# One stream of expert rows through all steps, and three latent input blocks moved ahead of the context's attention in layer 1

## The chip, the cores and the metric

One core of a Trainium2 chip runs the whole kernel in one launch. The metric is device time in microseconds (us), lower is better. Engines are named as in the profile: PE (TensorE, its weight loads apart as PEld), DVE (VectorE), ACT (ScalarE), POOL (GpSimd), SP (SyncE, which here only issues transfers).

## The reference, cut to what matters

Two layers over five blocks of 128 tokens (block 0 is the context, 1 to 4 are latent tokens), all in float32. In each layer every block goes through an input projection, four groups of attention or mixing heads, an output projection, a normalisation, and then PEER, the part this case is about: each token is routed to 16 of 16384 experts in each of 8 heads, and two gathered vectors of 1024 numbers, u and v, are used per expert.

```
h = x * (1 + scale1) + shift1 ; z = h @ w_in ; mix in four head groups
x = LayerNorm(alpha * x + gate1 * (GroupRMSNorm(concat) @ w_out))
h = x * (1 + scale2) + shift2
  s   = (h @ peer_w_q) . sub_keys ; top 16 of 128 twice, top 16 of 256 sums -> eid, gate
  act = gelu(peer_u[eid] . h)                          # per token, head, expert
  y   = sum over heads and experts of gate * act * peer_v[eid]
x = LayerNorm(alpha * x + gate2 * y)
```

Context tokens see only context keys, latent tokens see the latent blocks and a cached context.

## The kernel before, in words

**Steps.** The program is a chain of steps, each a block of five engine programs that ends in a barrier of all engines which also clears the semaphores (`end_step`, L379). mod(L) computes the modulation of layer L, in(L,b) the input projection of block b, att(L,b) the attention, output projection and routing of block b. The order is written out by hand at the end of `build`: mod(0), in(0,0), att(0,0), then per layer in(L,1) to in(L,4), att(L,1) to att(L,4), and between the layers mod(1), in(1,0), att(1,0). After the last att stands a step of experts alone, then the last sum.

**Expert rows.** Work on the experts of block b of layer L (a job) is 256 rows: 8 heads with 16 u rows and 16 v rows. A row is one gather of 128 x 1024 numbers (512 KB), issued by POOL (L502), which lands in a slot. A u row is reduced against the block's x2 by DVE (L603); 16 of them make a head's dots, ACT takes the gelu (L538) and DVE the weights (`wsel`, L596). Of the v rows DVE adds the odd ones into `acc` (L613), and PE the even ones into two PSUM banks (L571) with a diagonal matrix that ACT writes (L545). So of 256 rows DVE handles 192 and PE 64.

**How rows are mixed into a step.** Each step is handed some rows of a job (class `Experts`), and each engine's program calls `rows(share)` at fixed places between its own instructions; there it handles rows up to that share of the step's rows, in 256ths. POOL calls it too, and issues gathers as many rows ahead as there are slots: 8 in mod and in (`RING`), 16 in att (`DEEP`, where 8 more lie in W). A gather waits until the row that held its slot has been used, by DVE or by PE. Engines run their programs in order, so a place in the program is also a place in a queue.

**Which rows in which step, before.** in(L,1) to in(L,4) take one head of job 0 each (32 rows), att(L,1) the other four heads (128 rows), att(L,2) to att(L,4) the whole of jobs 1 to 3 (256 rows each). Job 4 of layer 0 is spread over mod(1) (64), in(1,0) (32) and att(1,0) (160); that of layer 1 fills the step of experts alone (256). In steps with fewer than 8 heads the rows come in blocks (16 u, then 16 u and 16 v by turns); with 8 heads u and v rows alternate after the first 16 u rows, and the last 16 are all v. Every step starts with no row gathered and ends with all of its rows used. A job's last sum (`last_sum`, L434: ten DVE instructions) is run at the start of the next step that begins a job, at head 1 in att (`experts_vector_ended`).

Of the kernel before, what the change touches and what calls it, by code (L numbers as in the profile page):

```python
# [12 lines left out]
ds = bass.ds  # L13
# [48 lines left out]
DIAGS = 4  # L62

# [10 lines left out]
def row_order(heads, turn):  # L74


    u = [("u", h, k) for h in range(heads) for k in range(TOPK)]
    v = [("v", h, k) for h in range(heads) for k in range(TOPK)]
    order, u = u[:TOPK], u[TOPK:]
    while v:  # L80
        order += u[:turn] + v[:turn]
        u, v = u[turn:], v[turn:]
    return order


# [4 lines left out]
class Experts:  # L90

    def __init__(self, layer, block, first, heads, begin=False, end=False, ended=None, slots=RING, landings=None):
        self.layer, self.block, self.first, self.heads = layer, block, first, heads
        self.begin, self.end, self.ended = begin, end, ended  # L100
        self.order = row_order(heads, 1 if heads == PH else TOPK)

        self.by_dve, self.by_pe = [], []
        d = p = 0
        for kind, _, k in self.order:
# [7 lines left out]
        self.slots = slots  # L113
        self.count = []
        for r in range(len(self.order)):
            landings[r % slots] += 16
            self.count.append(landings[r % slots])

    def target(self, share):

        return min(len(self.order), len(self.order) * share // 256)

    def landed(self, n):

        return self.count[n]


def build(nc, a):
    es = ExitStack()
    with es:  # L130
# [55 lines left out]
        gates_e = sb("gates_e", [P, NSEL])  # L186
        eid_e = sb("eid_e", [P, NSEL], U32)
        eid_s = sb("eid_s", [P, 4, TOPK], U32)
# [158 lines left out]
        ids_in = sem("ids_in")  # L347
        e_in = sem("e_in")
        x2_copied = sem("x2_copied")
        ids_staged = sem("ids_staged")  # L350
        acc_zero = sem("acc_zero")
        used_dve = sem("used_dve")
        used_pe = sem("used_pe")
        gelu_sel = sem("gelu_sel")
        w_ready = sem("w_ready")
        diag_done = sem("diag_done")
# [9 lines left out]
        bias_stored = es.enter_context(nc.semaphore("bias_stored"))  # L366
        gath = [es.enter_context(nc.semaphore(f"gathered{i}")) for i in range(DEEP)]
        landings = [0] * DEEP

        def slot(E, r):  # L370

            i = r % E.slots
            return ring[:, i, :] if i < RING else W[:, KD * D + (i - RING) * D:KD * D + (i - RING + 1) * D]
# [44 lines left out]
        def experts_sync(sp, E):  # L418
            if E is not None and E.begin:
                sp.dma_start(eid_e[:, :], of_block(eid_dram, E.block)).then_inc(ids_in, 16)  # L420
                if E.ended is not None:
                    last_sum_in(sp, E.layer, E.ended, ended_tiles)
                sp.dma_start(x2e[:, :], of_block(x2_dram, E.block)).then_inc(e_in, 16)
                sp.dma_start(gates_e[:, :], of_block(gate_dram, E.block)).then_inc(e_in, 16)

        def last_sum_in(sp, layer, block, tiles):

            s = 0 if isinstance(block, int) and block == 0 else 1
# [5 lines left out]
        def last_sum(dve, tiles):  # L434

            link = chain(dve, end_chain)
            link(dve.tensor_tensor(acc[:, :], acc[:, :], acc_ps, ALU.add))
            dve.wait_ge(end_in, 64)
            link(dve.tensor_tensor(acc[:, :], acc[:, :], tiles[1], ALU.mult))
            link(dve.scalar_tensor_tensor(acc[:, :], tiles[0], ALPHA, acc[:, :], ALU.mult, ALU.add))  # L440
            layer_norm(link, dve, acc[:, :], tiles[2], tiles[3], tiles[0], st12e, mve, vee[:, :], rstde[:, :],
                       end_var, end_rstd, 1).then_inc(end_done, 1)
# [5 lines left out]
        def experts_sync_ended(sp, E):  # L448

            if E is not None and E.ended is not None:  # L450
                sp.wait_ge(end_done, 1)
                sp.dma_start(of_block(x_dram, E.ended), ended_tiles[0]).then_inc(end_stored, 16)

        def experts_gpsimd_ended(pool, E):
            if E is not None and E.ended is not None:
                last_sum_rstd(pool)

        def experts_vector_ended(dve, E):
            if E is not None and E.begin:
                if E.ended is not None:  # L460
                    last_sum(dve, ended_tiles)

                    dve.wait_ge(end_done, 1)

                dve.memset(acc[:, :], 0.0).then_inc(acc_zero, 1)

        def experts_sync_end(sp, E):
            if E is None:
                return
            if E.end:  # L470

                sp.wait_ge(used_dve, E.by_dve[-1])
                sp.wait_ge(used_pe, E.by_pe[-1])
                tiles = [ring[:, i, :] for i in range(4)]
                last_sum_in(sp, E.layer, E.block, tiles)
# [1151 lines left out]
```

## Time and profile before

| what | value |
|---|---|
| device time, median of 3 runs | 5282.86 us (5281.63 to 5284.09) |
| time of the profiled execution | 5288.4 us |
| its span, first to last instruction | 5286.6 us |
| busy share of the span | DVE 65%, PE 57%, POOL 53%, ACT 12% |
| gathers | 2560, 512 KB each |

No engine is busy all of the time: the steps are chains in which engines wait for one another. The table of steps among the rows below is the place to start. Its stretches are the steps, cut at the barrier between the last instruction of one step and the first of the next.

### The profile page before, as it was taken

The page shows a single profiled execution, that of the slowest core. Times are in us where ns is not written, and L with a number is a line of the kernel's source. Part 1 is how long each engine was busy: PE and PEld are TensorE (multiplying, and loading weights), DVE is VectorE, ACT ScalarE, POOL GpSimd, SP SyncE. Part 2 cuts the span into 40 slices and gives each one's busy share as a digit, 9 for nine tenths or more (in the row PEclk, how much of TensorE's full clock was granted, in tenths as well). Part 3 has the DMA queues.
Part 4 walks back from the last instruction along what each step waited for, and adds up shares of the span by engine and source line. Part 5 has one row for each costly group of instructions (what it writes and reads, how often), then busy time and mean ns, then how long its engine had stood idle before and what let it go on. Part 6 is the DMA issues. An engine that isn't in the chain of part 4 may idle for free. (4 is left out here: it accounts for less than half of the span.)

```text
span 5286.6 us, 34528 instructions
## 1 busy us (share of the span) xinstructions
PE 3032.0 (57%) x9560; PEld 1575.4 (30%) x9560; DVE 3434.8 (65%) x6877; ACT 633.4 (12%) x1577; POOL 2815.9 (53%) x2837
## 2 busy tenths in 40 slices
PE   7638766366356546547554676645554663565354
PEld 1423344134133223311232333423332331332111
DVE  1255467677776866773568555667686677769775
ACT  0101121120121111000110001111111201211000
POOL 1116645366466646644654564445664664665675
PEclk8768868678678767778777786777776886787676
DMA  8447778789899988989896878769898998998998
GB/s 337 159 184 247 250 281 339 292 334 390 309 346 356 352 328 329 393 313 368 325 361 259 307 242 305 286 259 348 343 377 316 337 391 305 339 358 345 355 404 322
DMA packets 439839, 1690.09 MB, mean 320 GB/s; under 512 B 53120, under 2 KB 66496, under 8 KB 427568
## 3 DMA queue, kind: packets, MB, share of 16 engines
q0 software_dynamic: 370528, 1353.39, 67.7%
q1 hardware_dynamic: 69120, 334.49, 16.4%
q8 instruction: 79, 1.29, 0.1%
q14 instruction: 112, 0.92, 0.1%
HBM read 1660.02 MB, written 33.95 MB: 320 GB/s over the span
## 5 line engine op out<-in xcount | busy, mean ns | idle before, releaser
L571 PE MATMUL ps<-ring,diag 128*128 128x512 f32 x1456 | 875.8, 747 | 844.8 <-ACT diag L545 748.7
L502 POOL DMA_INDIRECT ring<-in_peer_u,eid_s x728 | 785.8, 1079 | 596.0 <-DVE dots L603 360.0
L502 POOL DMA_INDIRECT ring<-in_peer_v,eid_s x728 | 737.8, 1013 | 487.1 <-PE ps L571 217.7
L502 POOL DMA_INDIRECT W<-in_peer_v,eid_s x552 | 570.4, 1033 | 349.7 <-issue 125.9
L571 PE MATMUL ps<-W,diag 128*128 128x512 f32 x1104 | 618.8, 698 | 234.2 <-DMA W<-in_peer_v,eid_s 164.6
L603 DVE CUSTOM_DVE_ANT_0 ring<-ring,ps 128x1024 f32<-128x1024 f32 x552 | 658.4, 1217 | 142.4 <-DMA ring<-in_peer_u,eid_s 139.5
L603 DVE CUSTOM_DVE_ANT_0 W<-W,ps 128x1024 f32<-128x1024 f32 x552 | 655.6, 1217 | 102.0 <-DMA W<-in_peer_u,eid_s 100.7
L571 PEld LDWEIGHTS ps<-ring,diag 128*128 128x128 f32 x1456 | 320.7, 235 | 1296.8 <-issue 1126.0
L502 POOL DMA_INDIRECT W<-in_peer_u,eid_s x552 | 540.5, 979 | 292.6 <-DVE dots L603 130.1
L613 DVE SCALAR_TENSOR_TENSOR acc<-ring,wsel,acc 128x1024 f32<-128x1024 f32 x364 | 474.2, 1303 | 99.1 <-DMA ring<-in_peer_v,eid_s 69.5
L613 DVE SCALAR_TENSOR_TENSOR acc<-W,wsel,acc 128x1024 f32<-128x1024 f32 x276 | 354.8, 1286 | 50.0 <-DMA W<-in_peer_v,eid_s 24.7
L571 PEld LDWEIGHTS ps<-W,diag 128*128 128x128 f32 x1104 | 224.3, 218 | 544.2 <-issue 295.8
L869 PE MATMUL ps<-W,hT 128*128 128x512 f32 (+1 forms) x800 | 324.2, 567 | 31.4 <-DVE hT L999 22.1
L1210 PEld LDWEIGHTS ps<-hT,W 128*128 128x128 f32 x2560 | 298.1, 193 | 49.6 <-issue 34.0
L1210 PE MATMUL ps<-hT,W 128*128 128x128 f32 x2560 | 300.6, 277 | 19.4 <-ACT hT L1267 10.4
L545 ACT ACTIVATE diag<-ident,wsel 128x128 f32<-128x128 f32 x640 | 229.0, 398 | 684.6 <-PE ps L571 427.9
L603 DVE CUSTOM_DVE_ANT_0 ring<-ring,x2e 128x1024 f32<-128x1024 f32 x176 | 219.1, 1283 | 87.7 <-DMA ring<-in_peer_u,eid_s 86.7
L493 POOL COPY eid_s<-eid_e 128x16 uint32<-128x16 uint32 x80 | 23.7, 296 | 414.2 <-DMA eid_e<-expert_ids 332.7
L1158 PE MATMUL ps<-ktB,xs 64*128 64x512 f32 x64 | 49.3, 1130 | 331.2 <-DMA xs<-spill_state 202.3
L869 PEld LDWEIGHTS ps<-W,hT 128*128 128x128 f32 x800 | 151.5, 203 | 193.3 <-issue 168.0
L750 PE MATMUL ps<-W,condS 128*2 128x512 f32 x384 | 173.2, 612 | 48.6 <-DMA toep<-in_b_ada 48.6
L1324 DVE SCALAR_TENSOR_TENSOR big<-ps,toep 128x512 f32<-128x512 f32 x32 | 22.1, 689 | 249.9 <-DMA band<-in_c_band 207.4
(212 smaller groups left out, 3311.5 us busy)
## 6 DMA issues: line engine op xcount, KB each, us to landing
W<-in_w_q SPq DMA_DIRECT2D x40, 2048.0 KB
W<-in_w_ada SPq DMA_DIRECT2D x24, 2048.0 KB
W<-in_w_out SPq DMA_DIRECT2D x10, 4096.0 KB, 30.5
W<-in_w_in SPq DMA_DIRECT2D x16, 2048.0 KB, 10.1
ring<-in_peer_u,eid_s POOLq DMA_INDIRECT x728, 6.7
ring<-in_peer_v,eid_s POOLq DMA_INDIRECT x728, 6.3
toep<-mod_rows SPq DMA_DIRECT2D x20, 512.0 KB, 8.7
aux<-mod_rows SPq DMA_DIRECT2D x19, 512.0 KB, 5.7
```

What stands on the lines that cost most here:

```text
L493: pool.tensor_copy(eid_s[:, h % 4, :], eid_e[:, ds((E.first + h) * TOPK, TOPK)]).then_inc(ids_staged, 1)
L502: pool.indirect_dma_start(slot(E, r), None, a["peer_u"] if kind == "u" else a["peer_v"], bass.IndirectOffsetOnAxis(ap=eid_s[:, h % 4, k:k ...
L545: act.activation(diag[:, n % DIAGS, :], ident[:, :], ACT.Copy, scale=wsel[:, h % 2, k:k + 1]).then_inc(diag_done, 1)
L571: last = pe.matmul(acc_ps[:, c * 512:(c + 1) * 512], diag[:, (E.by_pe[r] - 1) % DIAGS, :], slot(E, r)[:, c * 512:(c + 1) * 512], start=Fal ...
L603: dve.tensor_tensor_reduce(out=slot(E, r), in0=slot(E, r), in1=x2, scale=1.0, scalar=0.0, op0=ALU.mult, op1=ALU.add, accum_out=dots[:, h % ...
L613: dve.scalar_tensor_tensor(acc[:, :], slot(E, r), wsel[:, h % 2, k:k + 1], acc[:, :], ALU.mult, ALU.add).then_inc(used_dve, 1)
L750: last = pe.matmul(bank(c % NB, parts=2), condS[:, k, :], ada[:, c % NB, k, :], start=(k == 0), stop=(k == KD - 1))
L869: last = pe.matmul(bank(c, n), hT[:, k, :], w_in[c][:, k, :], start=(k == 0), stop=(k == KD - 1))
L1158: pe.matmul(near(i, lat), q, k[:, k0 * P:k0 * P + lat], start=True, stop=True)
L1210: last = pe.matmul(bank(2 + i % 2)[:, g * P:(g + 1) * P], w_q[c][:, k, g * P:(g + 1) * P], hT[:, k, :], start=(k == 0), stop=(k == KD - 1))
L1324: dve.scalar_tensor_tensor(sS[:, i % 2, 0:lat], near(i, lat), sc, bias, ALU.mult, ALU.add)
```

## The change

One stream holds the rows of all ten jobs, in one order for all: per job 16 u rows, then u and v by turns, then the last 16 v rows. A step takes a slice of the stream, and a slice may hold the end of one job and the start of the next. At a step's end POOL goes on and issues the gathers of the next 8 rows (16 from one att to the next, and into the step of experts alone), as far as their block is routed; these gathers are under way across the barrier, and their semaphores and counts are no longer cleared by it. The slots are handed out beforehand, to the row whose turn comes, least recently used first.

| step | rows before | rows now |
|---|---|---|
| in(0,1) to in(0,4) | 32 each | 40 each |
| att(0,1) | 128 | 80 |
| att(L,2) to att(L,4) | 256 each | 256 each, 16 rows behind the job |
| mod(1) | 64 | 72 |
| in(1,0) | 32 | 40 |
| in(1,1), in(1,2), in(1,3) | 32 each, of job (1,0) | 40 each, of job (0,4), between in(1,0) and att(1,0) |
| att(1,0) | 160 | 40 |
| in(1,4) | 32 | 40 |
| att(1,1) | 128 | 200 |
| experts alone | 256 | 272 |

The last sum is cut into pieces that stand between the rows behind the job's end. The zeroing of `acc` (a memset, four matmuls) goes: the first v rows of a job overwrite. POOL no longer copies a head's expert numbers to `eid_s`. In(1,1) to in(1,3) use the input weights that lie in W from in(1,0); in(1,4) now loads them, which in(1,1) did.

```diff
+class Stream:
+    JOB = PH * HEAD_ROWS
+    def __init__(self, jobs):
+        one = [("u", h, k) for h in range(PH) for k in range(TOPK)]
+        two = [("v", h, k) for h in range(PH) for k in range(TOPK)]
+        order = one[:LEAD]
+        for i in range(len(two)):
+            order += one[LEAD + i:LEAD + i + 1] + two[i:i + 1]
...
+    def place(self):
+        self.slot, self.landed, self.prev = [], [], []
+        user, count = [-1] * DEEP, [0] * DEEP
+        for i, S in enumerate(self.slices):
+            from_shallow = i == 0 or not self.slices[i - 1].deep
+            for r in range(S.start, S.end):
+                wide = S.deep and not (from_shallow and r < S.start + RING)
+                at = min(range(DEEP if wide else RING), key=lambda n: (user[n], n))
...
+        self.limit = min(self.end + ahead, stream.JOB * routed)
...
+        def experts_gpsimd(pool, S):
...
+            def rows(share):
+                t = S.target(share)
+                while pool_at[0] < S.limit and stream.prev[pool_at[0]] < t:
+                    r = pool_at[0]
+                    j, kind, h, k = rows_of[r]
+                    if r == stream.first(j):
+                        pool.wait_ge(ids_in, 16 * (j + 1))
+                    p = stream.prev[r]
+                    if p >= 0:
+                        _, q, _, qk = rows_of[p]
+                        if on_pe(q, qk):
+                            pool.wait_ge(used_pe, by_pe[p])
                         else:
-                            pool.wait_ge(used_dve, E.by_dve[r - E.slots])
+                            pool.wait_ge(used_dve, by_dve[p])
...
+                    if S.ended is not None and r == stream.last(S.ended) and not S.at_end:
+                        ending[0] = last_sum(dve, S.ended, ended_tiles)
+                    if ending[0] is not None:
+                        next(ending[0], None)
...
-            step_input(L, 1, False, True, Experts(L, 0, 0, 1, begin=True, landings=landings))
...
-                step_attend_route(L + 1, 0, True, True, Experts(L, LAST, 3, PH - 3, end=True, slots=DEEP, landings=landings))
+                step_modulation(L + 1, next(part))
+                step_input(L + 1, 0, True, True, next(part))
+                for b in range(1, LAST):
+                    step_input(L + 1, b, False, False, next(part))
+                step_attend_route(L + 1, 0, True, True, next(part), shares=5)
```

On POOL, in(0,2) and in(0,3) stood as follows before: the 8 first gathers wait for nothing, the next 12 wait only for DVE, then come the two rstd and the rotation (L956 to L961), which the step's own chain needs.

```order
L502 DMA ring<-in_peer_u,eid_s 128x1024 [waits ids_staged]
L502 DMA ring<-in_peer_u,eid_s 128x1024 x7
L502 DMA ring<-in_peer_u,eid_s 128x1024 [waits used_dve] x8
L502 DMA ring<-in_peer_v,eid_s 128x1024 [waits used_dve] x4
L968 TENSOR_TENSOR rstd<-ve,neg_half 128x2 [waits var_done]
```

Now 15 gathers stand ahead of the first rstd there, and every fourth of them waits for PE; the last of them, up to the rstd (L1022 is L968 of before):

```order
L546 DMA ring<-in_peer_v,eid_e 128x1024 [waits used_pe]
L546 DMA ring<-in_peer_u,eid_e 128x1024 [waits used_dve]
L546 DMA ring<-in_peer_v,eid_e 128x1024 [waits used_dve]
L546 DMA ring<-in_peer_u,eid_e 128x1024 [waits used_dve]
L546 DMA ring<-in_peer_v,eid_e 128x1024 [waits used_pe]
L546 DMA ring<-in_peer_u,eid_e 128x1024 [waits used_dve]
L1022 TENSOR_TENSOR rstd<-ve,neg_half 128x2 [waits var_done]
```

What moved: the rstd has come behind gathers that wait for PE, and no gather of the step is free at its start. Between the two rstd stand 7 gathers (6 before), between the second and the last rotation 5 (4 before), and behind the last rotation 13 (2 before), 8 of which belong to the next step.

On DVE, head 1 of att(0,2) held the whole last sum before (its score rows stand ahead, the memset of `acc` closes it), and nine u rows behind it:

```order
L437 TENSOR_TENSOR acc<-acc,ps 128x1024
L439 TENSOR_TENSOR acc<-acc,aux 128x1024
L440 SCALAR_TENSOR_TENSOR acc<-aux,acc 128x1024
L405 BN_STATS st12e<-acc 128x6 x2
L406 BN_AGGR mve<-st12e 128x2
L407 TENSOR_SCALAR vee<-mve 128x1
L409 TENSOR_SCALAR acc<-acc,mve,rstde 128x1024
L410 TENSOR_TENSOR acc<-acc,aux 128x1024
L411 TENSOR_TENSOR aux<-acc,aux 128x1024
L465 MEMSET acc 128x1024
```

Now head 1 holds four v rows (PE has five), and the last sum's pieces begin in head 2, each behind a row:

```order
L1387 TENSOR_SCALAR small<-small 128x1
L665 SCALAR_TENSOR_TENSOR acc<-ring,wsel,acc 128x1024 x2
L665 SCALAR_TENSOR_TENSOR acc<-W,wsel,acc 128x1024 x2
L1397 RECIPROCAL small<-small 128x1
L1399 TENSOR_SCALAR aux<-ps,small 128x64
L1373 SCALAR_TENSOR_TENSOR big<-ps,toep 128x512
L1374 TENSOR_SCALAR big<-ps 128x128
L1375 TENSOR_REDUCE small<-big 128x1
L1387 TENSOR_SCALAR small<-small 128x1
L665 SCALAR_TENSOR_TENSOR acc<-W,wsel,acc 128x1024 x2
L473 TENSOR_TENSOR acc<-acc,ps 128x1024
L652 ISA ring,dots<-ring,ps 128x1024
```

What moved: the first 16 rows of such a step are now v rows, half of them PE's, where they were u rows, all DVE's; in return its last 16 rows, at the end of the routing, are u and v by turns, where they were v rows.

## Rows read from the trace of the kernel before

**Rows 1.** The page: span, and busy us of each engine (share, instructions).

```profile
span 5286.6 us, 34528 instructions
PE 3032.0 (57%) x9560; PEld 1575.4 (30%) x9560; DVE 3434.8 (65%) x6877; ACT 633.4 (12%) x1577; POOL 2815.9 (53%) x2837
```

**Rows 2.** Windows by step: length; PE, PEld, DVE, ACT, POOL busy; PEclk, DMA share, GB/s.

```profile
166.00:338.80 172.80, 75.87 (x396) 58.12 (x396) 76.62 (x288) 17.44 (x52) 18.18 (x6) 0.66 0.33 127
338.80:430.50 91.70, 58.13 (x161) 28.76 (x161) 42.79 (x77) 8.11 (x20) 42.11 (x47) 0.79 0.83 317
...
502.70:574.70 72.00, 56.24 (x157) 27.89 (x157) 41.09 (x75) 6.83 (x19) 47.99 (x47) 0.88 0.72 250
...
646.30:952.00 305.70, 180.74 (x692) 114.91 (x692) 206.44 (x480) 49.11 (x115) 131.34 (x134) 0.71 0.75 284
...
1406.70:1864.10 457.40, 246.45 (x824) 134.45 (x824) 331.23 (x655) 62.00 (x152) 262.73 (x267) 0.76 0.91 344
...
2320.30:2511.70 191.40, 124.53 (x271) 31.36 (x271) 78.60 (x112) 7.38 (x19) 83.73 (x67) 0.82 0.94 373
...
2584.90:2914.00 329.10, 152.95 (x556) 89.37 (x556) 230.04 (x503) 40.16 (x104) 166.90 (x168) 0.71 0.83 318
...
3220.50:3529.70 309.20, 183.62 (x692) 116.50 (x692) 206.43 (x480) 49.11 (x115) 131.55 (x134) 0.71 0.74 281
...
4899.20:5255.50 356.30, 185.27 (x260) 60.94 (x260) 244.44 (x339) 27.09 (x74) 261.00 (x265) 0.72 0.99 386
```

**Rows 3.** Windows of 10 us around the barrier at 1406.7 (att(0,2), att(0,3)).

```profile
1396.00:1406.00 10.00, 0.07 (x1) 0.00 (x0) 9.44 (x11) 0.00 (x0) 0.00 (x0) 0.74 0.04 13
1416.00:1426.00 10.00, 0.30 (x2) 0.31 (x4) 0.00 (x0) 1.02 (x1) 7.56 (x9) 0.50 1.03 381
```

**Rows 4.** Timeline around that barrier: start, length, what, [idle before <-releaser].

```profile
1384.97 2.02 POOL L502 DMA_INDIRECT W<-in_peer_v,eid_s  x1 [0.30 <-issue]
...
1409.60 0.97 POOL L502 DMA_INDIRECT ring<-in_peer_u,eid_s  x1 [0.27 <-POOL eid_s L493]
...
1434.98 0.69 DVE L1324 SCALAR_TENSOR_TENSOR big<-ps,toep 128x512 f32<-128x512 f32 x1 [28.77 <-DMA band<-in_c_band]
...
1469.89 2.04 PE L1158 MATMUL ps<-ktB,xs 64*128 64x512 f32 x2 [18.97 <-DVE aux L1350]
```

**Rows 5.** Queue of SP's loads from 1407 to 1435: packets, MB, share of 16 engines.

```profile
q1 hardware_dynamic: 2028, 4.65, 44.6%
```

**Rows 6.** Timeline of in(0,3), from the barrier at 502.7: PE, POOL, DVE.

```profile
511.66 25.50 PE L869 MATMUL ps<-W,hT 128*128 128x512 f32 x64 [2.74 <-DVE hT L999]
...
513.86 1.98 POOL L502 DMA_INDIRECT ring<-in_peer_u,eid_s  x1 [0.30 <-issue]
534.74 0.74 POOL L968 TENSOR_TENSOR rstd<-ve,neg_half 128x2 f32<-128x2 f32 x1
551.96 0.59 POOL L981 TENSOR_TENSOR rstd<-ve,neg_half 128x1 f32<-128x1 f32 x1
562.70 0.45 POOL L961 TENSOR_TENSOR big<-xs,aux 128x128 f32<-128x128 f32 x1
567.18 0.94 POOL L502 DMA_INDIRECT ring<-in_peer_v,eid_s  x1 [0.30 <-issue]
...
563.21 5.45 DVE L613 SCALAR_TENSOR_TENSOR acc<-ring,wsel,acc 128x1024 f32<-128x1024 f32 x4 [0.21 <-DVE big L1045]
572.26 1.28 DVE L613 SCALAR_TENSOR_TENSOR acc<-ring,wsel,acc 128x1024 f32<-128x1024 f32 x1 [3.60 <-DMA ring<-in_peer_v,eid_s]
```

**Rows 7.** Groups of PE and POOL in in(0,3): count, busy us, mean ns, idle before.

```profile
L571 PE MATMUL ps<-ring,diag 128*128 128x512 f32 x32 | 16.4, 659 | 8.3 <-ACT diag L545 8.3
...
L502 POOL DMA_INDIRECT ring<-in_peer_u,eid_s x16 | 21.1, 1318 | 5.1 <-issue 4.6 <-POOL eid_s L493 0.5
L502 POOL DMA_INDIRECT ring<-in_peer_v,eid_s x16 | 15.9, 994 | 11.0 <-PE ps L571 6.8 <-issue 4.0 <-POOL xs L961 0.3
```

**Rows 8.** Timeline of the end of att(1,0): the last sum's first instruction.

```profile
2893.41 1.22 DVE L437 TENSOR_TENSOR acc<-acc,ps 128x1024 f32<-128x1024 f32 x1
```

More of the change, by code:

```diff
@@ L62 @@
 DIAGS = 4
+LEAD = TOPK
 SHARES = {
@@ L70 @@
 }
[L74 to L83, printed above, removed]
 def on_pe(kind, k):
     return kind == "v" and k % BY_PE == 0
[L90 to L101, printed above, removed]
+class Stream:
[6 more added lines that the diff above has]
+            order += one[LEAD + i:LEAD + i + 1] + two[i:i + 1]
+        assert len(order) == self.JOB
+        self.rows = [(j,) + row for j in range(jobs) for row in order]
         self.by_dve, self.by_pe = [], []
         d = p = 0
-        for kind, _, k in self.order:
+        for _, kind, _, k in self.rows:
             if on_pe(kind, k):
@@ L458, in experts_vector_ended, with experts_sync_end @@
[L458 to L468, printed above, removed]
+                sp.dma_start(of_block(x_dram, JOBS[S.ended][1]), ended_tiles[0]).then_inc(end_stored, 16)
+        def experts_sync_end(sp, S):
+            if S is None or S.ended is None:
@@ L512, in finish @@
+                        bass.IndirectOffsetOnAxis(ap=eid_e[:, j % 2, h * TOPK + k:h * TOPK + k + 1], axis=0)).then_inc(gath[stream.slot[r]], 16)
+                    pool_at[0] += 1
+                    if pow_due[0] and pool_at[0] == stream.last(S.ended) + 1 + RSTD_AT:
+                        pow_due[0] = False
+                        last_sum_rstd(pool)
+            rows(0)
             def finish():
                 rows(256)
-                if E.end:
+                if S.at_end:
                     last_sum_rstd(pool)
+                assert not pow_due[0] and pool_at[0] >= S.end
@@ L529, in rows, with experts_scalar @@
+        def experts_scalar(act, S):
+            if S is None:
+                return lambda share: None
+            if not S.deep:
+                x2_held[0] = None
+            else:
+                r = stream.next_u(S.start)
+                if r < S.end and x2_held[0] != rows_of[r][0]:
+                    x2_to_psum(act, rows_of[r][0], r)
             def rows(share):
-                while at[0] < E.target(share):
-                    r = at[0]
-                    kind, h, k = E.order[r]
+                while act_at[0] < S.target(share):
+                    r = act_at[0]
+                    j, kind, h, k = rows_of[r]
+                    g = j * PH + h
@@ L1061, in step_attend_route @@
             G = 2 * PH
-            HEAD_SHARE, tail, q_share, route_share = SHARES[E.heads if E is not None else PH]
+            HEAD_SHARE, tail, q_share, route_share = SHARES[shares]
             A_END = NH * HEAD_SHARE
@@ L1471, in _ @@
                     rows, finish = experts_gpsimd(pool, E)
-                    experts_gpsimd_ended(pool, E)
+                    for share in range(4, 256, 4):
+                        rows(share)
                     finish()
```

360 lines of the change are left out of this document (196 added, 164 removed).

## The prediction

> **What bounds the kernel now.** The page first: no engine is busy throughout, DVE most with 3434.8 of 5286.6 us [rows 1]. So I cut the span at the barriers and read each step by itself [rows 2]; the reader should see four kinds of step. (a) The step of experts alone: 256 rows in 356.3 us, DMA share 0.99 at 386 GB/s. It is bound by the transfers, at about 1.35 us a row. (b) att with 256 rows: 457.4 us, DMA share 0.91, DVE 331 of 457. (c) att with fewer rows: 305.7 and 309.2 us with 128, 329.1 with 160 (context), 172.8 with none (context). (d) in: 72.0 us with 32 rows, no engine full (PE 56, DVE 41, POOL 48), DMA share 0.72; 91.7 where 9 MB of weights are loaded as well.
>
> Then the seams. Before the barrier at 1406.7 the DMA share is 0.04, after it 1.03 [rows 3]. POOL's last gather is issued at 1385.0, 21.7 us before the barrier, the next one at 1409.6, and DVE's first instruction starts at 1435.0, held for 28.8 us by a load (`band`) that lands among 16 gathers [rows 4] and 4.65 MB of loads of its own queue [rows 5]. That seam is what the stream fills. In the in step I read POOL and PE side by side [rows 6], since there the step's own chain (rstd, rotation) stands in POOL's queue between the gathers.
>
> **The change part by part.** Times in an in step are counted from its barrier.
>
> *In steps with 40 rows.* Before: PE's projection starts at +9.0 and its first four chunks end at +34.5; POOL's first rstd is at +32.0, the second at +49.3, the last rotation ends at +60.5, the last gather is issued at +64.5 and used 5.1 us later; the step ends at 72.0 [rows 2, 6]. A gather takes POOL 0.94 us where nothing holds it up, with 0.30 us to the next [rows 6]. Now the 8 first rows are there, but POOL is not ahead: it can issue nothing until DVE has used a row, which in its program comes behind hT, so at about +10. Of the 15 gathers ahead of the first rstd the last but one waits for a slot that PE frees with its fourth row, and those four rows now stand between PE's first chunks, where none stood. A PE row is four matmuls, 16.4 / 8 = 2.05 us on the mean [rows 7]: 8.2 us, so the first rstd comes near +40. Not all of that lasts, since PE waited 8.3 us for weights further on [rows 7], which now are there; on the other hand one gather more stands ahead of the second rstd and one ahead of the last rotation, 1.24 us each. I take the last rotation 7.5 us late, near +68. Behind it stand 13 gathers where 2 stood: 13 x 1.24 = 16 us, to +84. The tail of before (the 5.1 us until the last row is used, and DVE) is saved in return, being inside those 16 us. So **+12 us**, seven times. Lower bound +5: were the rotation on time, 60.5 + 16 ends at 77. Upper bound +20: if each of the 20 u rows stretched a gather, below. In(0,1) and in(1,4) start with nothing gathered and issue 40 + 8 rows where they issued 32; their first half is bound by the weights: +14 each, bounds +8 and +22. Together 7 x 12 + 2 x 14 = **+112** (45 to 184).
>
> Here a rule of the Trainium skill speaks against the change. The rows: the 16 gathers of u rows took POOL 1318 ns on the mean, those of v rows 994 [rows 7], and single ones 1.98 us while DVE ran u rows back to back with x2 in SBUF [rows 6]. The Trainium skill ("SBUF — State Buffer", Who interferes with whom) says that a DVE instruction with two SBUF inputs contends with a GpSimd instruction that reads SBUF, and that the one that comes second waits for the whole of the other. By that each u row of an in step could hold up a gather. The trace agrees for u rows, but DVE's v rows have two SBUF inputs too, and the gather at +64.5, under four of them, took 0.94 us [rows 6]. The sum stays by the rows; the rule's outcome is a rival.
>
> *att(0,1), 128 to 80 rows.* The price of a row in att is read from steps that differ in rows: between the context's 0 and 160 rows (329.1 less 20.6 for the last sum at its end, from 2893.4 to the barrier at 2914.0 [rows 8], less 172.8 [rows 2]) it is 0.85 us; between 128 and 256 rows (457.4 - 305.7) it is 1.19 us, but that holds the longer start and the last sum of the 256 step, which I put at 20 us, without which it is 1.03. For few rows I take 0.8, since the routing's matmuls leave DVE idle for rows to fit in: 48 x 0.8 = **-38** (-30 to -57).
>
> *att(1,0), 160 to 40 rows.* 120 x 0.85 = **-102** (-90 to -115); the 20.6 us at its end stay.
>
> *att(1,1), 128 to 200 rows.* 72 x 0.99, between the two slopes: **+71** (58 to 86).
>
> *mod(1), 64 to 72 rows.* DMA share 0.94 at 373 GB/s [rows 2]: 4.2 MB more are 11 us, less 3 for its seams: **+8** (0 to 20). SP now waits for the last sum (in the third of twelve pieces) before it loads a piece; two loaded pieces cover that.
>
> *Experts alone.* 272 rows, 16 of which are gathered before: 256 gathers as before, the first again 3 us after the barrier for want of the next job's numbers. **0** (-5 to +5).
>
> *att(L,2) to att(L,4), six times.* This decides. Start: without 16 gathers in front the loads have the transfers to themselves; 4.65 MB at 386 GB/s [rows 2, 5] are 12 us; with some 3 us until the first moves (the first gather is issued at +2.9 [rows 4]) and, as an estimate, 3 to 4 for the gathers still under way, DVE starts at +18 or 19, not +28.3: -10. Behind DVE's start both versions are alike, 16 rows gathered and 240 to come as slots are freed, so the lead does not grow. Then the order: the last 16 rows of a step are now three quarters DVE's, not half, and they stand in the routing, where DVE was 9.44 of 10 us busy up to the end [rows 3]: 4 x 1.28 = +5. At its start DVE has 4 instructions fewer, and PE's 19 us wait for DVE's last sum and nine u rows goes [rows 4], but PE gets 8 rows in two heads, some 3.6 us each (2.05 us at the in step's mean clock of 0.88 [rows 2, 7], scaled to the 0.50 that is granted there [rows 3], its 1.2 GHz level): nothing gained. POOL must issue the last freed slots' gathers behind DVE's last row: +2. The memset is 1 us. **-2 each, -12** (bounds -20 each, the whole seam, and +8, no earlier start).
>
> Sum: 112 - 38 - 102 + 71 + 8 + 0 - 12 = +39. The profiled execution took 5288.4 us, which would become 5327; the median of the runs is 5282.9, 5.5 below it, so **5322 us**. What the measurement tells from no change is 0.2%, 10.6 us.
>
> **The rivals.**
>
> *Transfers bind att: faster.* If in (b) the transfers and not the static order of DVE and PE set the pace, then filling the seam gives back all of it: 16 rows x 1.35 = 21 us per att. For it: DMA share 0.91 with the seam inside, so about 0.95 without. Against it: DVE is full behind the routing, and POOL is ahead there. Price (21 - 2) x 6 = 114 less: **5208**. It decides from about 11 us gained per att: the other terms sum to +51.
>
> *In steps absorb the rows.* If PE's four rows cost its chain nothing, for the 8.3 us that it waited [rows 7], and the rstd stay on time, in steps cost +5: 7 x 7 = 49 and about 14 in the other two, 63 less: **5259**. For it: that wait. Against it: 13 gathers behind the last rotation cost 16 us in either case.
>
> *Gathers held up by u rows.* In steps keep x2 in SBUF, and POOL's gathers beside their u rows take 1.98 us, not 0.94 [rows 6]. 20 u rows x (1.98 - 0.94) = 21 us per in step at most; POOL waits elsewhere for part of it, so 7: 9 x 7 = 63 more, **5385**. Against it: before, 16 u rows cost 16 x (1318 - 994) = 5 us [rows 7]. The rule behind it is that of the Trainium skill named above ("SBUF — State Buffer", Who interferes with whom).
>
> *The barrier waits for what is under way.* No gather crossed a barrier before, so no row shows it. If POOL's part of it waits until transfers have landed, each of the 18 seams with gathers under way costs up to 5.1 us [rows 6]: +92, **5414**.
>
> **How the numbers follow.** My sum 0.47 (its own range 5270 to 5365, from half the bounds of in and att: faster 0.02, same 0.07, slower 0.38). Transfers bind 0.17, all faster. In steps absorb 0.17 (faster 0.11, same 0.04, slower 0.02). Held-up gathers 0.13, slower. Barrier 0.06, slower. So faster 0.30, same 0.11, slower 0.59. The range 5200 to 5400 leaves out half of the transfers' case (0.08), most of the barrier's (0.05) and a third of the held-up gathers' (0.04).
>
> **What would show it.** In steps of 40 rows near 84 us, POOL's first rstd near +40, 13 gathers back to back behind the last rotation; an in step of 77 or less falls with that step. att with 256 rows near 455, DVE's first instruction at +18 or 19 and its last row just ahead of the barrier; 440 or less is the first rival. att(0,1) near 268, att(1,0) near 227, att(1,1) near 380. If the first gathers of a step have all landed at the barrier, and POOL sits in it, it is the fourth. The prediction fails if the att steps give back more than 11 us each, or if prices per row taken from steps with rows in blocks don't hold for rows by turns.

## The result, and the profile after

The changed kernel takes 5572.9 us (median of 4 runs, 5570.8 to 5575.2), the kernel before beside it 5283.5: ratio 1.0545, 95% interval 1.0527 to 1.0563. The forecast was 5322, slower by 39; it is slower by 289. The profiled execution has a span of 5569.0 us, 282 more than before. By steps, in the columns of [rows 2] (windows cut at the barriers):

```profile
340.00:456.00 116.00, 57.28 (x149) 27.55 (x149) 53.38 (x98) 7.53 (x18) 64.94 (x62) 0.72 0.85 323
554.70:655.00 100.30, 63.82 (x165) 30.53 (x165) 48.52 (x86) 7.65 (x21) 58.86 (x54) 0.79 0.64 222
...
755.50:1048.70 293.20, 151.06 (x644) 99.12 (x644) 162.87 (x418) 43.12 (x101) 96.58 (x90) 0.70 0.63 224
...
1515.80:1987.70 471.90, 251.57 (x820) 138.71 (x820) 329.51 (x654) 63.63 (x154) 273.08 (x259) 0.73 0.89 333
2441.00:2653.30 212.30, 127.81 (x275) 30.79 (x275) 83.98 (x122) 6.89 (x20) 91.17 (x73) 0.81 0.91 356
3051.20:3272.80 221.60, 103.27 (x452) 68.33 (x452) 116.37 (x337) 25.14 (x70) 33.13 (x35) 0.69 0.45 170
...
3387.60:3785.40 397.80, 212.54 (x764) 121.59 (x764) 270.75 (x572) 58.81 (x139) 221.40 (x210) 0.75 0.86 324
```

In order: in(0,1), in(0,3), att(0,1), att(0,3), mod(1), att(1,0), att(1,1). The in step has 100.3 us where 72.0 stood in [rows 2] and 84 in the forecast; att with 256 rows 471.9 where 457.4 stood; its DMA share fell from 0.91 to 0.89 although the seam was to be filled.

The seam between att(0,2) and att(0,3) says why. Its timeline (compare [rows 4]):

```profile
1501.51 1.28 DVE L665 SCALAR_TENSOR_TENSOR acc<-W,wsel,acc 128x1024 f32<-128x1024 f32 x1
...
1506.49 0.94 POOL L546 DMA_INDIRECT W<-in_peer_v,eid_e  x1 [0.30 <-issue]
1516.36 0.32 SPq L452 DMA_DIRECT2D eid_e<-expert_ids  x1
...
1533.30 0.69 DVE L1373 SCALAR_TENSOR_TENSOR big<-ps,toep 128x512 f32<-128x512 f32 x1 [30.50 <-DMA band<-in_c_band]
```

DVE uses the step's last row up to 1502.8; POOL goes on issuing gathers for the next step up to 1507.4; then nothing runs until the barrier at 1515.8. Then DVE starts 17.5 us behind it, not 28.3 as in [rows 4]: that half of the forecast came, and 13 us of waiting stand in front of it. No row of the timeline fills them, since instructions of the sequencer are not among its rows. The view of one source line has them. L1157 opens the step's block, and its end belongs to it; the columns are operation, count, duration in ns (least, median, most), first and last start:

```profile
L1157 SPq DRAIN  x1: 7/7/7, 1499.2 to 1499.2; - x1
...
L1157 POOLq DRAIN  x1: 12467/12467/12467, 1502.8 to 1502.8; - x1
```

POOL executes a DRAIN at the end of a step. Its record begins at 1502.8, as DVE's last row ends, and lasts to 1515.3; SP's took 0.007 us, DVE's and ACT's had ended by 1503, and these engines stand at the barrier. POOL's last gather, issued at 1506.5, lands 6.3 us later, at 1512.8; the DRAIN ends 2.5 us behind that. The time to landing, from the view of the gathers' line between 1506 and 1516 (its last two gathers):

```profile
DMA to landing us min/median/max: 6.3/6.3/6.3
```

The same DRAIN was there before (L1104 of att(0,2), at the barrier at 1406.7):

```profile
L1104 POOLq DRAIN  x1: 13582/13582/13582, 1379.8 to 1379.8; - x1
```

It took 13.6 us there as well, but ended at 1393.4, 13 us ahead of the barrier, under DVE's routing. It also ended 6.4 us behind POOL's last gather (1384.97 and 2.02 us long [rows 4]). The prediction's "no row shows it" was wrong: the view of that line bears on it, and the prediction had read the timeline alone.

The in step: PE, DVE and POOL in in(0,3), from the timeline, to be held against [rows 6]:

```profile
565.20 3.75 PE L618 MATMUL ps<-ring,diag 128*128 128x512 f32 x4 [4.55 <-ACT diag L598]
...
576.22 1.88 PE L618 MATMUL ps<-ring,diag 128*128 128x512 f32 x4
...
594.29 0.74 POOL L1022 TENSOR_TENSOR rstd<-ve,neg_half 128x2 f32<-128x2 f32 x1
...
603.96 0.15 DVE L1083 TENSOR_SCALAR ve<-mv 128x1 f32<-128x1 f32 x1
...
612.06 0.94 POOL L546 DMA_INDIRECT ring<-in_peer_v,eid_e  x1 [0.31 <-issue]
613.01 3.78 PE L618 MATMUL ps<-ring,diag 128*128 128x512 f32 x4 [4.83 <-DMA ring<-in_peer_v,eid_e]
613.02 0.59 POOL L1035 TENSOR_TENSOR rstd<-ve,neg_half 128x1 f32<-128x1 f32 x1
...
616.23 1.29 DVE L665 SCALAR_TENSOR_TENSOR acc<-ring,wsel,acc 128x1024 f32<-128x1024 f32 x1
616.41 1.96 POOL L546 DMA_INDIRECT ring<-in_peer_u,eid_e  x1 [2.79 <-DVE dots L652]
...
618.68 1.94 POOL L546 DMA_INDIRECT ring<-in_peer_v,eid_e  x1 [0.30 <-DVE dots L652]
...
626.90 1.32 POOL L1015 TENSOR_TENSOR big<-xs,aux 128x128 f32<-128x128 f32 x1
628.37 1.79 POOL L546 DMA_INDIRECT ring<-in_peer_v,eid_e  x1 [0.15 <-issue]
...
639.80 1.22 DVE L652 CUSTOM_DVE_ANT_0 ring<-ring,x2e 128x1024 f32<-128x1024 f32 x1 [2.29 <-DMA ring<-in_peer_u,eid_e]
639.86 1.97 POOL L546 DMA_INDIRECT ring<-in_peer_v,eid_e  x1 [0.30 <-issue]
642.14 0.94 POOL L546 DMA_INDIRECT ring<-in_peer_u,eid_e  x1 [0.30 <-issue]
642.56 1.28 DVE L665 SCALAR_TENSOR_TENSOR acc<-ring,wsel,acc 128x1024 f32<-128x1024 f32 x1 [1.53 <-DMA ring<-in_peer_v,eid_e]
643.38 1.28 POOL L546 DMA_INDIRECT ring<-in_peer_v,eid_e  x1 [0.30 <-issue]
...
646.20 0.94 POOL L546 DMA_INDIRECT ring<-in_peer_v,eid_e  x1 [0.30 <-issue]
```

From the barrier at 554.7: first rstd at +39.6 (forecast +40), second at +58.3, end of the last rotation at +73.5 (forecast +68), 13 gathers to +92.4 (forecast +84), and 7.9 us more to the barrier. Those 7.9 us are the DRAIN again. Here the last gather takes 6.4 us to land, at 652.6, and the DRAIN (to 654.3) ends 1.7 us behind it:

```profile
DMA to landing us min/median/max: 6.4/6.4/6.4
```

```profile
L866 POOLq DRAIN  x1: 10404/10404/10404, 643.9 to 643.9; - x1
```

A gather that starts just behind the start of a DVE row is held (1.96 and 1.97 us), one that starts ahead of it is not (0.94 at 642.14).

Step lengths of the kernel before, of the forecast, and of the changed kernel with its variants, from the profiled executions (us; "in" is the mean of the seven steps of the prediction's first term, "in w" of the two that load weights as well, in(0,1) and in(1,4) (in(1,1) before), "att 256" of the six):

| kernel | time | in | in w | att(0,1) | att(1,0) | att(1,1) | att 256 | mod(1) |
|---|---|---|---|---|---|---|---|---|
| before | 5283.5 | 71.9 | 91.8 | 305.7 | 329.2 | 309.2 | 456.3 | 191.4 |
| forecast | 5322 | 84 | 106 | 268 | 227 | 380 | 454 | 199 |
| after | 5572.9 | 99.6 | 115.4 | 293.1 | 221.6 | 397.7 | 465.4 | 212.4 |
| a1, no DRAIN | 5447.0 | 92.0 | 105.1 | 291.1 | 228.6 | 387.7 | 458.3 | 201.0 |
| a2, nothing ahead | 5494.4 | 89.5 | 104.5 | 284.4 | 232.4 | 380.2 | 468.2 | 211.8 |
| a4, 32 rows in in | 5507.2 | 86.0 | 104.3 | 313.6 | 250.2 | 396.0 | 465.9 | 210.5 |
| b1, a1 and a4 | 5379.9 | 79.2 | 93.4 | 314.0 | 252.8 | 390.2 | 458.5 | 199.2 |
| c3, a1 and 24 rows | 5333.1 | 70.8 | 79.8 | 327.6 | 271.4 | 399.2 | 459.9 | 201.0 |
| b2, a2 and 2 rows behind | 5500.1 | 89.3 | 104.5 | 298.9 | 215.2 | 395.0 | 472.4 | 202.5 |
| b3, half ahead | 5508.0 | 94.2 | 110.0 | 289.1 | 224.2 | 380.5 | 464.3 | 211.1 |

### The profile page after: what moved, and what is told of

The parts are those of the page before. It is cut to its first block and busy times, and to the rows that moved or that the text cites. A ratio compares the mean times of both kernels' runs of the same rounds, so it can differ in the third digit from the quotient of the medians.

```text
span 5569.0 us, 34531 instructions
## 1 busy us (share of the span) xinstructions
PE 3047.2 (55%) x9520; PEld 1575.4 (28%) x9520; DVE 3416.1 (61%) x6867; ACT 637.3 (11%) x1585; POOL 2892.7 (52%) x2757
## 5 line engine op out<-in xcount | busy, mean ns | idle before, releaser
L618 PE MATMUL ps<-ring,diag 128*128 128x512 f32 x1488 | 912.5, 753 | 642.7 <-ACT diag L598 376.7
L546 POOL DMA_INDIRECT ring<-in_peer_u,eid_e x760 | 798.6, 1051 | 846.3 <-DVE dots L652 414.7
L546 POOL DMA_INDIRECT ring<-in_peer_v,eid_e x744 | 814.5, 1095 | 621.7 <-PE ps L618 318.8
L618 PE MATMUL ps<-W,diag 128*128 128x512 f32 x1072 | 659.2, 754 | 558.2 <-ACT diag L598 439.0
L546 POOL DMA_INDIRECT W<-in_peer_v,eid_e x536 | 580.4, 1083 | 412.5 <-PE ps L618 178.2
L546 POOL DMA_INDIRECT W<-in_peer_u,eid_e x520 | 524.7, 1009 | 419.1 <-issue 147.0
L652 DVE CUSTOM_DVE_ANT_0 ring<-ring,ps 128x1024 f32<-128x1024 f32 x528 | 630.6, 1216 | 101.5 <-DMA ring<-in_peer_u,eid_e 99.7
L652 DVE CUSTOM_DVE_ANT_0 W<-W,ps 128x1024 f32<-128x1024 f32 x520 | 621.3, 1216 | 98.1 <-DMA W<-in_peer_u,eid_e 95.8
L652 DVE CUSTOM_DVE_ANT_0 ring<-ring,x2e 128x1024 f32<-128x1024 f32 x232 | 292.3, 1278 | 133.0 <-DMA ring<-in_peer_u,eid_e 132.0
L1399 DVE TENSOR_SCALAR aux<-ps,small 128x64 f32<-128x64 f32 x120 | 34.0, 283 | 239.9 <-PE ps L1231 238.3
```

The costliest lines, as they stand in the source:

```text
L546: pool.indirect_dma_start(row_tile(r), None, a["peer_u"] if kind == "u" else a["peer_v"], bass.IndirectOffsetOnAxis(ap=eid_e[:, j % 2, h * ...
L618: last = pe.matmul(acc_ps[:, c * 512:(c + 1) * 512], diag[:, (by_pe[r] - 1) % DIAGS, :], row_tile(r)[:, c * 512:(c + 1) * 512], start=open ...
L652: dve.tensor_tensor_reduce(out=row_tile(r), in0=row_tile(r), in1=x2, scale=1.0, scalar=0.0, op0=ALU.mult, op1=ALU.add, accum_out=dots[:, g ...
L1399: dve.tensor_scalar_mul(ob[:, GW + i * HD:GW + (i + 1) * HD], out_of(i), small[:, 48 + i:49 + i]).then_inc(pv_used, 1)
```

## The experiments

**The DRAIN left out (a1).** The step's end then goes by semaphores alone, in the steps that hold rows. The barrier's own DRAINs on the five engines go too; they took 0.007 to 0.047 us each at the seam above.

```diff
-        def end_step():
-
-            nc.all_engine_barrier(sems_to_clear=all_sems)
+        def end_step(drain=True):
+
+            if drain:
+                nc.all_engine_barrier(sems_to_clear=all_sems)
+            else:
+                nc.gpsimd.sem_clear(all_sems)
+                nc.all_engine_barrier(sem_only=True)
...
-            with nc.Block() as block:
+            with nc.Block(no_gpsimd_drain=E is not None) as block:
...
-            end_step()
+            end_step(E is None)
```

> The changed kernel, with POOL's DRAIN at the end of every step that hands rows on left out (the barrier then goes by semaphores alone); rows, order and gathers as they are. Theory (drain): the 10 to 14 us at the end of a step in which only POOL's DRAIN is under way are a wait for the transfers under way. From the end of POOL's last gather to the barrier there are 6.9 to 10.0 us at 17 seams, 139 us in all, of which about 1 each belongs to any barrier: 122 less, 5451 us. If the loads at a step's start then share the transfers with those gathers, up to 5 us at each of 8 seams in front of an att come back: 5490. Rival (rows): what costs is the rows themselves and their order in the in steps, and the wait would only move into the next step: above 5540 us.

5447.0 us, ratio to before 1.0301 (1.0284 to 1.0318): 126 less than the changed kernel, where 122 were expected. The same seam:

```profile
1465.49 1.28 DVE L669 SCALAR_TENSOR_TENSOR acc<-W,wsel,acc 128x1024 f32<-128x1024 f32 x1
...
1467.96 0.32 SPq L456 DMA_DIRECT2D eid_e<-expert_ids  x1
...
1470.47 0.95 POOL L550 DMA_INDIRECT W<-in_peer_v,eid_e  x1 [0.30 <-issue]
...
1489.02 0.69 DVE L1377 SCALAR_TENSOR_TENSOR big<-ps,toep 128x512 f32<-128x512 f32 x1 [22.25 <-DMA band<-in_c_band]
```

SP now issues the next step's loads 1.2 us behind DVE's last row, while POOL is still issuing gathers, and DVE's idle time from step to step falls from 30.5 to 22.3 us: 8 of the 13 us stay, the rest comes back, since DVE now starts 21.7 us behind the barrier, not 17.5. The rival that the wait only moves falls.

**The DRAIN left out of the kernel before (a3).** The same edit on the other kernel.

> The kernel before, with POOL's DRAIN left out at the end of the same steps. Theory (drain): in att with 256 rows its DRAIN began 27 us before the barrier and took 13.6, so it ended long before DVE; only in the in steps it ended with DVE's last row. So 0 to 15 us less: 5268 to 5283. Rival (a DRAIN costs its own 8 to 14 us wherever it stands): 18 times 8, below 5150.

5288.5 us, ratio 1.0000 (0.9989 to 1.0011). In that kernel the DRAIN is hidden, since it ends ahead of the step's last work or together with it, and it costs nothing.

**One spare gather across the barrier, in the kernel before (c1, c2).** At the end of the six att steps with 256 rows POOL waits for the last row's use, then gathers one row that nobody reads; the next step's first gather waits until it has landed. c2 does so without the DRAIN.

```diff
+            if E.spare_landed:
+                pool.wait_ge(gath[0], E.spare_landed)
             gather_until(E.slots)
...
                 rows(256)
+                if E.spare:
+                    pool.wait_ge(used_dve, E.by_dve[-1])
+                    pool.wait_ge(used_pe, E.by_pe[-1])
+                    pool.indirect_dma_start(
+                        ring[:, 0, :], None, a["peer_v"],
+                        bass.IndirectOffsetOnAxis(ap=eid_s[:, 3, 15:16], axis=0)).then_inc(gath[0], 16)
```

> The kernel before with one gather more at the end of the six att steps with 256 rows: POOL waits until DVE and PE have used the last row, then gathers one row into a free slot, which nobody reads. Nothing else of the stream. Drain theory: each of those six barriers now waits for that gather: 0.9 us to issue it, 5.1 until it has landed, about 1.5 until the DRAIN ends, 7 to 8 us a step, 45 in all: about 5333 us. Rival (a barrier does not care what is under way): within 8 us of the kernel before.

> The same spare gathers, without POOL's DRAIN at the end of the steps. Drain theory: only the 0.9 us of the issue are left, 6 in all, and some contention at the next step's start: 5285 to 5300 us. Rival (a gather that lands across a barrier costs as much wherever it is waited for): as the run with the DRAIN.

With the DRAIN 5329.6 us, ratio 1.0082 (1.0065 to 1.0099); without it 5280.7, ratio 0.9982 (0.9973 to 0.9992). So a DRAIN that stands behind the step's last row, with one gather under way, costs a barrier some 7 us, in a kernel that has nothing else of the change. The seam of att(0,2) in c1, first the timeline, then the DRAIN of the block's line:

```profile
1412.00 2.67 DVE L625 SCALAR_TENSOR_TENSOR acc<-W,wsel,acc 128x1024 f32<-128x1024 f32 x2
1414.94 0.94 POOL L523 DMA_INDIRECT ring<-in_peer_v,eid_s  x1 [19.49 <-DVE acc L625]
1422.73 0.32 SPq L424 DMA_DIRECT2D eid_e<-expert_ids  x1
```

```profile
L1116 POOLq DRAIN  x1: 6881/6881/6881, 1414.7 to 1414.7; - x1
```

The gather's landing is in the view of transfers (KB where known, then us from issue to landing):

```profile
ring<-in_peer_v,eid_s POOLq DMA_INDIRECT x1, 4.1
```

It lands at 1419.1, and the DRAIN ends at 1421.6, 2.5 us behind the landing: the rival in the prediction had the 5.1 us of [rows 6] and not this tail. In all six seams of c1 the DRAIN ends 2.5 us behind the landing.

c1 does two things at once: it puts a gather under the DRAIN, and it moves the DRAIN from 27 us ahead of the barrier to the step's end. No run has the second without the first. That the second alone would cost something shows in att(1,0) of the kernel before, where the last gather had landed 35 us earlier and the DRAIN still took 5.75 us:

```profile
L1104 POOLq DRAIN  x1: 5747/5747/5747, 2906.8 to 2906.8; - x1
```

**Nothing gathered ahead (a2), half as much ahead (b3).** The limit of a step's gathers, a2 first:

```diff
-        self.limit = min(self.end + ahead, stream.JOB * routed)
+        self.limit = self.end
...
+        self.limit = min(self.end + ahead // 2, stream.JOB * routed)
```

> The changed kernel without gathers across a barrier: each step issues the gathers of its own rows only; rows per step and their order as they are. Theory (drain): nothing is under way at a barrier, so the drain is hidden again; an in step has 5 gathers behind its last rotation, not 13, and ends near 88 us, not 100 (nine times 12); att with 256 rows ends near 458, since DVE starts 10 us later but waits for no drain (six times 9); mod(1) 10 less: about 5400 us. Rival (rows): in steps stay within 4 us of 100, and the time above 5530.

> The changed kernel with half as many gathers ahead: 4 across a barrier in front of in and mod, 8 in front of att. DRAIN stays. Drain theory: it waits for the last gather to land, and the last gather is now issued 4 or 8 rows earlier, so part of its landing lies beside DVE's last rows: in steps 6 us shorter (nine), att and mod 5 (nine): about 5470 us. Rival (a DRAIN with any gather under way has a length of its own): above 5550.

a2: 5494.4 us, 94 above what the drain theory gave. The in steps came nearly as expected (89.5); mod(1) did not (211.8, where some 202 were expected), nor did att with 256 rows: 468, not 458. DVE starts there 31 us behind the barrier, 2 later than before, and ends 12 later than before: without gathers ahead the stream is slower than the old steps by itself. b3: 5508.0 us, between the two expectations. In steps are 5.4 us shorter, as expected; att only 1.1, since the 8 gathers that are now issued behind the barrier delay DVE's start again, to 27 us. What the DRAIN gives back the start loses.

**Fewer rows in the in steps (a4, b1, c3).** 32 rows (a4), the same without the DRAIN (b1), and 24 rows without it (c3); the rows that leave go to att(0,1), att(1,0) and att(1,1).

```diff
-        IN_ROWS = 40
+        IN_ROWS = 32
```

> The changed kernel with 32 rows in the in steps, not 40; the 72 rows go to att(0,1) (112), att(1,0) (72) and att(1,1) (208). Prediction's prices: 8 gathers of 1.24 us less in nine in steps (-90), 72 rows at 0.85 to 0.99 more in att (+65): about 5548 us. If the in steps are longer because of the order (u and v by turns, PE's rows between its chunks) or the drain and not the number of rows, they stay above 96 us and the time rises to 5600 or more.

> Both edits at once: 32 rows in the in steps and no DRAIN of POOL's where rows are handed on. If the drain (-126 in the run without it) and the eight rows (-66) are separate costs, they add up: about 5375 to 5385 us, still above the kernel before, by the order of the rows alone (in steps 5 us and att 5 to 10 us longer than before). If they are one cost, seen twice, the time stays near 5445.

> The changed kernel without the DRAIN and with 24 rows in the in steps (32 there gave 5380); the other 72 rows go to att(0,1), att(1,0) and att(1,1). If a row of an in step keeps its price of 1.7 us, in steps fall from 78.5 to 65 us and the sum to 5380 - 9 x 13.5 + 72 x 0.95 = 5327. If the in steps have a floor near 72 us that rows fill for nothing, it is 5380 - 60 + 68, about 5390.

a4: 5507.2 us, 66 less than with 40 rows, where 25 were expected. b1: 5379.9, as expected: the two costs add up. c3: 5333.1, ratio 1.0077 (1.0061 to 1.0094), near the first of its two expectations, 5327, but by luck: the in steps fell to 70.8 us, not 65, and the 72 rows cost 41 us in att, not 68, and these misses mostly cancel. In an in step without the DRAIN, going from 40 to 32 rows saves 12.8 us, 1.6 a row; from 32 to 24 it saves 8.4, 1.05 a row. In att(0,1) the same rows cost 0.72 each from 80 to 112 and 0.43 from there to 144, in att(1,0) 0.76 and 0.58. Forty rows were past the point where the in step has room.

**Two rows behind, not 16 (b2).** With nothing ahead as in a2, so that u and v rows stand in att nearly as they did before.

```diff
-        TAIL_ROWS = TOPK
+        TAIL_ROWS = 2
...
-        MOD_ROWS = TAIL_ROWS + 56
+        MOD_ROWS = 72
```

> The changed kernel without gathers across barriers, and with 2 rows, not 16, of a job left to the next step (mod(1) keeps 72 rows): in att with 256 rows u and v rows then stand nearly where they stood before. Order theory: those att steps, 468 us without gathers ahead and 16 rows behind, come back to 457 to 460 us, and the whole to about 5440. Rival (the stream's own code: handed-out slots, the last sum in pieces, the copy of x2): they stay at 465 or more, the whole near 5490.

5500.1 us; att with 256 rows takes 472.4, more than with 16 rows behind, as the rival had it. The theory that the place of the 16 v rows alone makes the stream's att longer falls. What in the stream's code does it was not separated; one possible cost is read from the rows, below.

**An early start without the stream (b4, c4).** The kernel before, where POOL in att issues 4 gathers and holds the other 12 until the bias rows and `band` have landed (b4); then also those loads ahead of the expert inputs and the last sum's in SP's queue (c4).

```diff
+            if held:
+                gather_until(4)
+                pool.wait_ge(x_loaded, 32)
             gather_until(E.slots)
...
-                    rows, finish = experts_gpsimd(pool, E)
+                    rows, finish = experts_gpsimd(pool, E, not context)
```

c4 in addition, in SP's program of att:

```diff
-                    experts_sync(sp, E)
...
+                    if E is not None and E.begin:
+                        sp.dma_start(eid_e[:, :], of_block(eid_dram, E.block)).then_inc(ids_in, 16)
...
                         lay(band[:, :], a["c_band"][:, ds(NLAT * P - b * P, lat)], x_loaded)
+                    if E is not None and E.begin:
+                        sp.dma_start(x2e[:, :], of_block(x2_dram, E.block)).then_inc(e_in, 16)
+                        sp.dma_start(gates_e[:, :], of_block(gate_dram, E.block)).then_inc(e_in, 16)
+                        if E.ended is not None:
+                            last_sum_in(sp, E.layer, E.ended, ended_tiles)
```

> The kernel before with one wait more: in att of latent blocks POOL issues 4 gathers, then waits for the bias rows and the band that DVE's first instruction needs, and then issues the other 12. It does the early start of the changed kernel alone, without the stream and its order. If a start 8 to 10 us earlier is worth that in a step (as the prediction had it), eight steps give 64 to 80: about 5210 us. If the 12 gathers that come later hold DVE and PE up behind the start by as much, it stays within 15 us of 5285.

> The kernel before with the 12 gathers held back (that alone gave 5265), and with the loads for DVE's first instruction moved in SP's queue ahead of the expert inputs and the last sum's. DVE starts near 14 us in six att steps, not 22. If half of a start is kept, as in the run before, 6 x 4 less: 5240 us. If gathers and PE set the pace of att whatever DVE's start, 5260 to 5275.

b4: 5265.3 us, ratio 0.9955 (0.9937 to 0.9972), between its two expectations: DVE starts 6 us earlier, of which 2.4 a step stay. c4: 5208.2 us, ratio 0.9844 (0.9827 to 0.9861), better than both kernels and than either expectation. Its att(0,3), from the barrier at 1395.5, in the columns of [rows 2] and then DVE's first instruction:

```profile
1395.50:1841.80 446.30, 253.67 (x824) 137.44 (x824) 331.54 (x655) 61.89 (x152) 264.68 (x267) 0.74 0.92 352
```

```profile
1406.53 0.69 DVE L1332 SCALAR_TENSOR_TENSOR big<-ps,toep 128x512 f32<-128x512 f32 x1 [11.56 <-DMA band<-in_c_band]
```

DVE starts 11 us behind the barrier; over the six steps 13.5 of some 18 us stay. The seam of [rows 4] was worth filling from its near side, by the order of loads, with no gather across the barrier.

## Why the prediction was wrong, by its own steps

The direction was right and the size was not. Terms in us against the kernel before:

| term | forecast | after | a1 |
|---|---|---|---|
| in, seven | +84 | +194 | +141 |
| in w, two | +28 | +47 | +27 |
| att(0,1) | -38 | -13 | -15 |
| att(1,0) | -102 | -108 | -101 |
| att(1,1) | +71 | +89 | +79 |
| att 256, six | -12 | +54 | +12 |
| mod(1) | +8 | +21 | +10 |

The miss is 251 us (5573 against 5322), in two halves. Without the DRAIN 125 of it are left: +57 in the seven in steps, +24 in att with 256 rows, +23 in att(0,1), the rest small. No rival reached 5573, since each was priced alone and several came together.

**The step that failed first: the sum has nothing for the barrier.** The prediction had that wait as its fourth rival, "The barrier waits for what is under way", at a chance of 0.06 and 92 us. It holds: without the DRAIN 126 us go (a1), a late DRAIN over one spare gather costs the old kernel some 7 us a seam (c1), the same gather without the DRAIN costs nothing (c2), and where the DRAIN was hidden, leaving it out changes nothing (a3). The sign that the prediction named for it is there: at 1512.8 the last gather has landed, and POOL sits in the barrier to 1515.3. It was set low because no row was thought to bear on it; the DRAIN's row of 13.6 us was there. Its price was low because the last gathers took 6.3 and 6.4 us to land, not 5.1, and the DRAIN lasts 1.7 or 2.5 us more.

That the wait follows the landing is read from the trace: the DRAIN ends 1.7 us behind it in each of the seven in steps and 2.5 us behind it in five of the six att steps with 256 rows, while the landing itself came 4.8 to 5.7 us behind the end of POOL's last gather. How much would be left of the wait if every gather had landed, no run shows; att(1,0) says that it is not nothing. The Trainium skill ("PSUM — Partial Sum Buffer", Engine vs sequencer instructions) says that a drain waits for the engine to go fully idle; by that it should have had more weight. The trace agrees and goes further: POOL's last gather ended at 1507.4, and the DRAIN lasted to 1515.3, behind that gather's landing. "Perfetto Trace Analysis" of the Trainium skill (DMA Instruction — SWDGE (GPSIMD)) adds that such a gather's record ends with its descriptors, not with its data: in c1 0.94 us of record and 4.1 us to landing.

**In steps: the mechanism held, the size did not.** The first rstd at +39.6 and the 13 gathers behind the last rotation are as forecast. Without the DRAIN a step took 20 us more than before, not 12. The rotation ended at +73.5, for two reasons. The credit for PE's 8.3 us wait [rows 7] was not paid: between the first rstd and the second POOL's own queue sets the pace. DVE has the second rstd's input ready at 604.1, and POOL comes to it at 613.0, straight from its gathers. It was so before, at 545.5 and 552.0, so an earlier PE could not have helped there:

```profile
545.39 0.15 DVE L1030 TENSOR_SCALAR ve<-mv 128x1 f32<-128x1 f32 x1
```

And POOL took 4 us longer than before from the second rstd to the rotation's end, where 1.24 were forecast, with two held gathers, the first of which had waited 2.8 us for DVE. PE did wait anew, 4.6 us for a diagonal ahead of its first chunk and 4.8 for a gathered row behind its last; the first of these is inside the +39.6. The 13 gathers took 18.8 us, not 16. This is the rival "Gathers held up by u rows", behind the rotation at a third of its price or so, inside the sum and not in its place. The prediction had the rule behind it ("SBUF — State Buffer", Who interferes with whom, in the Trainium skill) hold for u rows only; the trace bears it out for v rows too, and as the Trainium skill has it, by who comes first: the gather at 616.41 started 0.18 us behind the start of a v row and took 1.96 us, the one at 642.14 started ahead of one and took 0.94. The 0.94 us in [rows 6] from which the prediction excused v rows was of that second kind: the last of the four v rows began 0.2 us behind it. The rival "In steps absorb the rows" falls. Of the 20 us, 13 are the eight rows beyond 32 (a1, b1): that term was mis-sized. The other 7 stand with 32 rows too, and are the order of the rows or what comes with it, not separated. (The prediction's lower bound for the in steps is 7 x 5 + 2 x 8 = 51, not 45; nothing hung on it.)

**att with 256 rows: the start came, the end did not.** DVE started at +17.5 (forecast +18 or 19) and ended its last row, on the mean of the six, only 1.6 us earlier than before (att(0,2): +454.1, before +454.2). Where the rest went shows in the groups of DVE's waits in the heads of att(0,2) (us in total, times, longest), first after, then before:

```profile
DVE aux L1399 <- PE ps L1231: 29.4, 7, 7.5
```

```profile
DVE aux L1350 <- PE ps L1178: 14.4, 3, 5.4
```

PE's 8 rows now stand in the first heads, between the step's own matmuls, and DVE waits 15 us longer for PE in the heads. The forecast named those rows and booked them as "nothing gained"; by these rows they were a loss, which no run tried by itself. Then POOL's last gathers came 4.6 us behind DVE's last row (forecast 2), and the DRAIN 8 more. Only att(0,4) escaped the DRAIN: it gathers 8 rows ahead with 16 slots, its last gather goes out while DVE still has rows, and the step took 453.3 us. The rival "Transfers bind att" falls: without the DRAIN the seam is filled (in a1 the DMA share is 0.95 to 1.11 from 1467 to 1490), and those att steps take 458 us, not 436.

**Prices per row.** att(1,0) at 0.85 was right, att(1,1) nearly. att(0,1) was not: with 112 rows of the stream it takes 314.0 us and with 144 327.6 (b1, c3), so some 321 with 128, where blocks took 305.7. The price of one row was near (0.72 against 0.8); the whole step is some 15 us longer by turns than in blocks, for a reason that no run separates. That is close to the failure the prediction named last, that prices from rows in blocks do not hold for rows by turns.

What stays open: the 12 us that the stream's att takes longer with nothing ahead (a2). PE's rows may be one cost, but not all of it: over the same 330 us of att(0,2) DVE waits 27.6 us for PE in a2 and 20.8 in b2, and b2's att steps are 4 us longer still.

## What to carry to other kernels

Before a transfer is let run across a barrier, look for what ends the barrier on each engine, in the sequencer's rows too: a wait that was always hidden is in the trace, and the change may uncover it. Price the last rows that are put into a step, not its mean row: the eight rows above 32 cost 1.6 us each in the in step and less than half of that in att(0,1). And ask whether the seam can be filled from the near side, by the order of loads, before work is carried across it.

## What was not expected of the hardware

A DRAIN on POOL lasts until the gathers that POOL issued have landed, and some time longer. That time goes with the number of gathers in the step, not with what is under way: 1.35 us with 32 (in steps before), 1.68 with 40 (in steps after, and in a2 with nothing ahead), 2.66 with 64 and 2.98 with 72 (mod(1), before and after). It does not go on growing: with 256 it is 2.49. With nothing under way the DRAIN of att(1,0) took 5.75 us in the kernel before (160 gathers) and 3.29 us in the changed one (32 in its own step). Its record begins before the last gathers of its own engine (1502.8 against 1506.5), so the record's start is no sign that POOL was done.
